# Differential attention prompt heads: a bank each for two small score blocks, the next block's maximum ahead of the mixture, and two buffers for a head's result

## What is computed

```python
def block(args):
    q_blk, i = args
    qpos = i * Q_BLOCK + jnp.arange(Q_BLOCK)
    s = jnp.einsum('bqhcd,bkhcd->bhcqk', q_blk, k, preferred_element_type=jnp.float32) * scale
    w = diff_weights(s, kpos[None, :] <= qpos[:, None], lam_full)      # softmax(s0) - lam * softmax(s1)
    return jnp.einsum('bhqk,bkhe->bqhe', w.astype(v.dtype), v)
...
o = rms_norm(o, subln_g) * (1.0 - lam_init)
return (o.reshape(B, T, ATTN_DIM) * jax.nn.silu(z)) @ w_out
```

## Time and profile before

| | |
|---|---|
| median of 3 runs | 2562.84 us (2559.9 to 2563.27) |
| the profiled execution | 2562.2 us, span 2560.4 us |
| heads 0 to 7 of the prompt | 2008.7 to 2265.7 us of the span |
| projection with the other 56 pages | 2265.7 to 2484.4 us |
| tail (rest of the projection, decode output) | 2484.4 to 2560.4 us |

### The profile page before, as it was taken

The page is one execution under the profiler, slowest core; times in us unless marked ns, Lnnn a source line. Parts: engine busy times, 40 slices in busy tenths (PEclk is TensorE's granted clock), DMA queues, the critical chain, the costliest instruction groups (busy, mean ns, idle before and its releaser), DMA issues.

```text
span 2560.4 us, 51030 instructions
## 1 busy us (share of the span) xinstructions
PE 2472.4 (97%) x20963; PEld 2164.5 (85%) x20963; DVE 1513.4 (59%) x1663; ACT 1016.2 (40%) x1832; POOL 347.5 (14%) x137
## 2 busy tenths in 40 slices
PE   8999999999999999999999999999999987789999
PEld 7999999999999999899999999998999532345565
DVE  4665675665664334455789878877667565643211
ACT  4111211111121223777655467776555334331111
POOL 4323332323321111000000000000000022120000
PEclk9999999999999999999999999999999988889999
DMA  5323323323323332234477787877888999989996
GB/s 155 83 82 97 84 82 91 90 82 87 93 82 87 106 118 91 94 108 159 141 257 271 259 280 245 287 269 265 286 299 295 354 366 388 372 305 376 380 343 221
DMA packets 376326, 520.52 MB, mean 203 GB/s; under 512 B 16553, under 2 KB 311858, under 8 KB 357682
## 3 DMA queue, kind: packets, MB, share of 16 engines
q1 hardware_dynamic: 314434, 461.55, 52.5%
q10 hardware_dynamic: 61600, 56.45, 6.5%
q0 software_dynamic: 128, 0.26, 0.0%
HBM read 483.46 MB, written 34.75 MB: 202 GB/s over the span
## 4 chain that ended last, share of the span: by engine, by line
PE 83%; DVE 5%; ACT 5%; DMA 4%; issue 2%; ACTq 1%; SPq 1%; POOL 0%; DVEq 0%; POOLq 0%
PE psum L112 25%; PE psum L1292 16%; PE psum L120 12%; PE psum L1300 8%; PE psum L1888 7%; PE psum L1343 4%; PE psum L1962 4%; ACT w_raw L1057 1%; DVE h_keys_turned L1235 1%; DMA w_raw<-in_w_in_b_dram 1%; PE psum L1941 1%; PE psum L1308 1%; PE psum L1923 1%; DMA w_raw<-in_w_kv_dram 1%; DVE prompt_probs L1779 1%
## 5 line engine op out<-in xcount | busy, mean ns | idle before, releaser
L1292 PE MATMUL psum<-x_hi,w_hi 128*128 128x272 f32 x2048 | 433.6, 293 | 0.0
L112 PE MATMUL psum<-x_hi,w_hi 128*128 128x272 f32 x2048 | 427.4, 289 | 2.2 <-DVEq L446 2.2
L112 PE MATMUL psum<-x_lo,w_hi 128*128 128x272 f32 x2048 | 426.5, 290 | 0.0
L1292 PE MATMUL psum<-x_lo,w_hi 128*128 128x272 f32 x2048 | 425.3, 289 | 0.0
L1292 PEld LDWEIGHTS psum<-x_hi,w_hi 128*128 128x128 f32 x2048 | 321.4, 189 | 16.6 <-issue 16.5
L112 PEld LDWEIGHTS psum<-x_hi,w_hi 128*128 128x128 f32 x2048 | 321.9, 190 | 2.7 <-issue 2.3
L1292 PEld LDWEIGHTS psum<-x_lo,w_hi 128*128 128x128 f32 x2048 | 321.4, 188 | 0.0
L112 PEld LDWEIGHTS psum<-x_lo,w_hi 128*128 128x128 f32 x2048 | 321.2, 189 | 0.0
L1235 DVE STREAM_TRANSPOSE h_keys_turned<-h_ring 128x1024 f32<-128x1024 f32 x256 | 299.9, 1215 | 22.0 <-DMA h_ring<-in_cache_k_dram 11.1
L399 POOL TENSOR_TENSOR w_raw<-w_raw,params 128x2048 f32<-128x2048 f32 x63 | 240.4, 3817 | 508.5 <-DMA w_raw<-in_w_in_a_dram 508.5
L1300 PE MATMUL psum<-x_hi,w_lo 128*128 128x272 f32 x2048 | 285.3, 294 | 0.0
(11 more groups left out here) (214 smaller groups left out, 3010.4 us busy)
## 6 DMA issues: line engine op xcount, KB each, us to landing
h_ring<-in_cache_k_dram SPq DMA_DIRECT2D x256, 512.0 KB, 6.7
ring<-in_cache_v_dram SPq DMA_DIRECT2D x128, 1024.0 KB, 8.1
w_raw<-in_w_in_a_dram SPq DMA_DIRECT2D x64, 1024.0 KB, 6.1
w_raw<-in_w_kv_dram SPq DMA_DIRECT2D x16, 2048.0 KB, 13.4
w_raw<-in_w_in_b_dram SPq DMA_DIRECT2D x15, 2048.0 KB, 10.0
w_raw<-in_w_out_a_dram SPq DMA_DIRECT2D x16, 1024.0 KB, 5.6
wo_raw<-in_w_out_b_dram SPq DMA_DIRECT2D x8, 2048.0 KB, 12.1
ring<-in_w_out_b_dram SPq DMA_DIRECT2D x16, 1024.0 KB, 7.2
```

The costliest lines, as they stand in the source:

```text
L112: pe.matmul(out[:, g, 0:GT], m.WH[s][:, k * P:(k + 1) * P], x[:, k * T + g * GT:k * T + (g + 1) * GT], start=(k == 0 and x is xh), stop=Fa ...
L1292: pe.matmul(psum[n % 2][:, g, 0:GT], m.WH[n % 2][:, k * P:(k + 1) * P], x[:, k * T + g * GT:k * T + (g + 1) * GT], start=(k == 0 and x is ...
```

## The change

Block 2's scores of both maps go side by side into bank 2 and block 3's into bank 3 (`scores_of`), so that blocks 1, 2 and 3 can be scored once block 0's exponentials are done, without waiting for each other; the next head's block 0 now waits for all exponentials of this head. Maxima, sums and inverses get a column pair for each block. Orders within a head are rewritten on all three engines: VectorE takes block `x + 1`'s maximum ahead of block `x`'s mixture; the next head's first scores move from step 7 to step 6 on TensorE; the sum of squares moves from step 1 to step 2; ScalarE's `norm_o` moves from step 1 to step 4 and `split_y` with `load_gate` from step 5 to step 8. `o` gets a second buffer in the space of the projection's first high weights, so `take_o(r)` waits for head `r - 2`; in return `split_hi(0)` and `split_lo(0)` move to step 8 of the last head, and `split_hi(0)` waits for GpSimd's end of head 6. The turned decode output (`turn_rows`, `take_out`) moves by up to three steps where it would meet the squares in their bank.

```diff
-        self.pmx, self.pden, self.pinv = work(2), work(2), work(2)
+        self.pmx, self.pden, self.pinv = ([work(2) for x in range(TT)] for a in range(3))
...
+    LAST_NORM = 2
...
-        def score_bank(x):
-            return (BB, A)[x % 2]
+        def scores_of(x):
+            n = (rows_of(x) + 1) * P
+            if x < 2:
+                return m.PS[:, (BB, A)[x]:(BB, A)[x] + 2, 0:n]
+            return m.PS[:, BB + x - 2, 0:2 * n].rearrange("p (c n) -> p c n", c=2)
...
+        def turned_at(i):
+            v = (i + 1) * NPG + 1
+            while any(squares_at(r) <= v <= squares_at(r) + (LAST_NORM if r < H - 1 else 0) for r in range(H)):
+                v += 1
+            return v
...
             def split_hi(n):
...
+                    if n == 0:
+                        act.wait_ge(yl_ready, H - 1)
...
             def head_step(r, j):                       # ScalarE
-                if j == 0 and r:
-                    load_inner(r + 1)
-                    square_o(r - 1)
-                if j == 0 and r == H - 1:
-                    split_hi(0)
+                if j == 0:
+                    if r:
+                        load_inner(r + 1)
+                        square_o(r - 1)
+                    prompt_exps(r, 1)
                 if j == 1:
                     prompt_weights(r, 0)
+                    prompt_exps(r, 2)
+                if j == 4:
+                    prompt_weights(r, 1)
+                    prompt_exps(r, 3)
                     if r:
                         norm_o(r - 1)
-                if j == 2:
-                    prompt_exps(r, 1)
-                if j in (4, 6):
-                    prompt_weights(r, j // 2 - 1)
-                    prompt_exps(r, j // 2)
-                if j == 5 and r:
-                    split_y(r - 1)
+                if j == 5:
+                    prompt_weights(r, 2)
                 if j == 7:
                     prompt_weights(r, 3)
-                if j == 8 and r + 1 < H:
-                    prompt_exps(r + 1, 0)
+                if j == 8:
+                    if r + 1 < H:
+                        prompt_exps(r + 1, 0)
+                    if r:
+                        split_y(r - 1)
+                    if r == H - 1:
+                        split_hi(0)
...
             def take_o(r):
                 dve.wait_ge(o_done, r + 1)
-                after(dve, yl_ready, r)
+                after(dve, yl_ready, r - 1)
...
             def head_step(r, j):                       # VectorE
                 if j == 0:
-                    prompt_mix(r, 0)
                     if r:
                         take_o(r - 1)
-                if j == 1 and r == H - 1:
-                    split_lo(0)
-                if j in (2, 4, 6):
-                    prompt_max(r, j // 2)
-                if j in (3, 5, 7):
-                    prompt_mix(r, j // 2)
-                if j == 8 and r + 1 < H:
+                    prompt_max(r, 1)
+                if j == 1:
+                    prompt_max(r, 2)
+                if j == 2:
+                    prompt_mix(r, 1)
+                if j == 3:
+                    prompt_max(r, 3)
+                if j in (4, 5):
+                    prompt_mix(r, j - 2)
+                if j == 6 and r + 1 < H:
                     prompt_max(r + 1, 0)
+                if j == 8:
+                    if r + 1 < H:
+                        prompt_mix(r + 1, 0)
+                    else:
+                        split_lo(0)
...
             def prompt_scores(r, x):
                 if x == 0:
                     pe.wait_ge(inner_in[r % 2], 48 * (r // 2 + 1))
-                    after(pe, prompt_exp, r * (2 * TT) - 2)
+                    after(pe, prompt_exp, r * (2 * TT))
...
                 else:
-                    pe.wait_ge(prompt_exp, r * (2 * TT) + 2 * (x - 1))
+                    pe.wait_ge(prompt_exp, r * (2 * TT) + 2)
...
             def head_step(r, j):                       # TensorE
+                if j == 0:
+                    prompt_scores(r, 1)
                 if j == 1:
-                    if r:
-                        prompt_turn(r, 0)
-                    prompt_scores(r, 1)
-                    if r:
-                        prompt_squares(r - 1)
-                if j == 2 and r == 0:
                     prompt_turn(r, 0)
-                if j in (3, 5):
-                    prompt_scores(r, (j + 1) // 2)
-                if j in (4, 6):
-                    prompt_turn(r, j // 2 - 1)
+                    prompt_scores(r, 2)
+                if j == 2 and r:
+                    prompt_squares(r - 1)
+                if j == 3:
+                    prompt_scores(r, 3)
+                if j == 4:
+                    prompt_turn(r, 1)
+                if j == 5:
+                    prompt_turn(r, 2)
+                if j == 6 and r + 1 < H:
+                    prompt_scores(r + 1, 0)
                 if j == 7:
                     prompt_turn(r, 3)
-                    if r + 1 < H:
-                        prompt_scores(r + 1, 0)
                 if j == 8:
                     prompt_out(r)
```

More of the change, by code:

```diff
@@ L1429, in attend_and_project @@
         yh, yl = sb("ay_hi", [P, KT * SEQ], F32R), sb("ay_lo", [P, KT * SEQ], F32R)
-        with nc.sbuf_tensor("wo_hi_first", [P, D], F32):
+        with nc.sbuf_tensor("o_early", [P, D], F32) as o_even:
             with nc.sbuf_tensor("norm_early", [P, D], F32) as early:
@@ L1433, in attend_and_project @@
         wh = [sb(f"wo_hi{s}", [P, D], F32R) for s in range(2)]
-        o = sb("prompt_o", [P, 1024])[:, :]
+        o_odd = sb("prompt_o", [P, 1024])
         with nc.sbuf_tensor("heads", [P, 7 * 1024], F32) as heads:
@@ L1447, in attend_and_project @@
         pwt = sb("prompt_weights", [P, 2048])[:, :]
+        o = [(o_even[:, 0:1024], o_odd[:, :])[r % 2] for r in range(H)]
         ro = [early[:, 1024:1536]] * (H - 1) + [pwt[:, 1536:2048]]
@@ L1503, in place, with squares_at @@
             return None, None, n, v - STARTS[n]
+        def squares_at(r):
+            return FIRST + 1 if r == H - 1 else (r + 1) * HP + 2
+        def turned_at(i):
[3 more added lines that the diff above has]
+            return v
         @block.sync
@@ L1638, in square_o @@
                 act.wait_ge(o_taken, r + 1)
-                act.activation(osq[r], o, ACT.Square).then_inc(osq_ready, 1)
+                act.activation(osq[r], o[r], ACT.Square).then_inc(osq_ready, 1)
             def norm_o(r):
@@ L1775, in prompt_mix @@
                 dve.wait_ge(prompt_exp, r * (2 * TT) + (2 * x + 2))
-                prompt.link(dve.reciprocal(pinv, pden))
-                prompt.link(dve.tensor_scalar(w[:, SEQ:SEQ + n], w[:, SEQ:SEQ + n], pinv[:, 1:2], m.NLAM[:, 0:1],
+                prompt.link(dve.reciprocal(pinv[x], pden[x]))
+                prompt.link(dve.tensor_scalar(w[:, SEQ:SEQ + n], w[:, SEQ:SEQ + n], pinv[x][:, 1:2], m.NLAM[:, 0:1],
                                               ALU.mult, ALU.mult))
-                dve.scalar_tensor_tensor(out=w[:, 0:n], in0=w[:, 0:n], scalar=pinv[:, 0:1], in1=w[:, SEQ:SEQ + n],
+                dve.scalar_tensor_tensor(out=w[:, 0:n], in0=w[:, 0:n], scalar=pinv[x][:, 0:1], in1=w[:, SEQ:SEQ + n],
                                          op0=ALU.mult, op1=ALU.add).then_inc(prompt_w, 1)
@@ L1823, in seq_step @@
             def seq_step(i, p):
-                if p == 2 and i:
+                if i and i * NPG + p == turned_at(i - 1):
                     take_out(i - 1)
@@ L1838, in _ @@
             prompt_max(0, 0)
+            prompt_mix(0, 0)
             for v in range(NV):
@@ L1905, in turn_rows @@
                 after(pe, out_taken, i)
-                after(pe, o_ln, 2 * min((i + 1) * NPG // HP, H) - 1)
+                after(pe, o_ln, 2 * sum(squares_at(r) <= turned_at(i) for r in range(H)) - 1)
                 for t in range(4):
@@ L1920, in prompt_scores @@
                 else:
-                    pe.wait_ge(prompt_exp, r * (2 * TT) + 2 * (x - 1))
+                    pe.wait_ge(prompt_exp, r * (2 * TT) + 2)
                 for c in range(2):
-                    last = pe.matmul(m.PS[:, score_bank(x) + c, 0:(qb + 1) * P], qh[r % 2][:, c * SEQ + qb * P:c * SEQ + (qb + 1) * P],
-                                     kh[r % 2][:, c * SEQ:c * SEQ + (qb + 1) * P], start=True, stop=True)
+                    last = pe.matmul(scores_of(x)[:, c, :], qh[r % 2][:, c * SEQ + qb * P:c * SEQ + (qb + 1) * P],
+                                     kh[r % 2][:, c * SEQ:c * SEQ + (qb + 1) * P], start=True, stop=True, skip_group_check=True)
                 last.then_inc(prompt_scored, 1)
@@ L1947, in prompt_squares @@
                 pe.wait_ge(osq_ready, r + 1)
-                after(pe, out_taken, ((r + 1) * HP - 1) // NPG)
+                after(pe, out_taken, sum(turned_at(i) < squares_at(r) for i in range(NSEQ)))
                 for e in range(2):
@@ L2004, in seq_step @@
             def seq_step(i, p):
```

(2 more changed lines are left out.)

21 lines of the change are left out of this document (10 added, 11 removed).

## The result

The changed kernel takes 2577.54 us in the median of 11 runs (2567.42 to 2586.89), against 2564.8 us (2557.73 to 2567.88) for the kernel before on the same chip: ratio 1.0051, 95% interval 1.0032 to 1.0069. It is slower by 0.5%, some 13 us. Forecast were 2548 us and a range that ended at 2562. The third rival, starvation, had the sign, with +8 us where some 13 were measured. The profiled execution is the slowest of the runs, 2586.89 us with a span of 2584.3, so its own differences to before are larger than those of the medians; what follows is read for where and why, and the sizes are taken from the timed runs.

The account below looks back on a forecast made before the run. The prediction took a latency chain through three engines to bound the heads, with DMA traffic right below it. Gains of 6.4 (heads 1 to 6), 3 (head 0) and 4.7 us (hand-over) took 2562.2 to 2548 us; range 2536 to 2562.

Parts of the forecast that it names:

- The third rival, starvation: Heads 1 to 6: pages crowd out gate and head data in the other queue; +8 us, 2570 us, chance 0.13.
- The chain bounds the kernel before: Heads before the change: a latency chain through three engines sets the time, 32.2 us a head.
- The chain alone would run at 24.5 us a head: Heads in the new order: without the DMA bound, about 24.5 us a head instead of 32.2.
- At least 176.1 us of DMA in heads 1 to 6: Heads 1 to 6: 74.48 MB at 423 GB/s take 176.1 us, so at most 17.3 us can go.
- TensorE will stand 5 to 9 us for the head's data in heads 1 to 5: Before the next head's first scores: values land after they are needed, so TensorE idles 5 to 9 us each time.
- 1.8 us of idle DMA a head: Heads 1 to 6: a third of the possible 5.5 us idle, giving 186.9 us, a gain of 6.4 us.
- The traffic, named as a sign at near 400 GB/s: Heads 1 to 6 after the change: DMA traffic was to show near 400 GB/s.
- Head 0 gains 3: Head 0: no finished head to carry, its order improves alike; gain 3 us (0 to 4).
- the first rival: Heads and hand-over: the chain gain comes through whole with no DMA idle; -27 us, 2535 us, chance 0.16.
- Head 7 and the hand-over gain 4.7: Last head to first projection matmul: the shorter chain counts, part lost to the weight split; gain 4.7 us.
- Projection and tail unchanged: Projection and tail: TensorE is full, its work is the same and DMA has room; no change.
- The range: Whole kernel: 2536 us (nearly the whole gain) to 2562 us (idle DMA of 3.9 us a head).

Follow-up runs that it names:

- e8: Kernel before, with only a quarter of each of 72 pages loaded and used four times: 2560.71 us, ratio 0.9987.
- e7: Changed kernel, with only a quarter of each of 72 pages loaded and used four times: 2547.5 us, ratio 0.9940.
- e5: Changed kernel, with queries, keys and values of heads 2 to 7 loaded in SyncE's page queue: 2554.69 us, ratio 0.9967.
- e12: Changed kernel, with head data in the page queue, `norm_o` at step 5 and `take_o(7)` before `split_lo(0)`: 2549.41 us, ratio 0.9952.
- e9: Changed kernel, with `take_o(7)` in front of `split_lo(0)` on VectorE: 2574.49 us, ratio 1.0047.
- e2: Changed kernel, with the next head's first scores and their maximum back at step 7: 2568.56 us, ratio 1.0028.
- e3: Changed kernel, with the gate's load issued behind the next head's queries, keys and values: 2576.5 us, ratio 1.0057.
- e10: Changed kernel, with `norm_o` behind weights 2 at step 5 instead of in front at step 4: 2579.14 us, ratio 1.0064.
- e1: Changed kernel, with values counted by their own semaphore, so first scores wait for queries and keys alone: 2559.06 us, ratio 0.9987.

## Why the prediction was wrong, point by point

*The chain bounds the kernel before.* Right: with light pages it stays where it was (e8), and the mixture of 384 columns fell from 2.335 us on average to 0.619. It did not stand behind GpSimd in every head, though: in head 0, which has no finished head to carry, it took 0.62 us before too, and 2.58 in the other seven.

*The chain alone would run at 24.5 us a head.* Too short by 5: e7 shows 29.3. This is a second error, and it made the first one dear. The plan had the chain 4.8 us a head below the DMA floor of 29.3, so a stall would have been half hidden; in truth the chain is as long as that floor, and the table above shows the long stalls added in full. Some heads do run at 23 to 25. In others `take_o` waits behind the decode softmax, and GpSimd's subtraction meets VectorE at step 8. The schedule had put the decode work down as 2 us of TensorE time and not as work in front of `take_o`.

*At least 176.1 us of DMA in heads 1 to 6.* Nothing went below it with all pages: 179.9 us in e5, at 414 GB/s, and 180.0 in e12. That it alone bounds these heads isn't shown, because with light pages the chain takes 175.5 us, nearly the same. The heads of e5 are within 0.9 us of those of e7 one by one, save 2.6 us in head 6. So single heads can run at 25 us with full pages, which the prediction thought forbidden; only their mean can't.

*TensorE will stand 5 to 9 us for the head's data in heads 1 to 5.* The place was right. The size was wrong in its pattern: in the profile 1.75 to 12.43 us in four heads and none in the others. Which heads stall differs from one execution to the next (2, 4 and 6 in e9's profile), but with this order and ScalarE's queue as it was head 6 is always among them: it takes 38 to 43 us in the profiles of the changed kernel, e2, e3, e9 and e10. The 11 runs spread over 19 us, where 6 of e5 spread over 4. That one stall brings on the next, by a ring that is refilled beside the head's data, fits this but isn't shown by itself.

*1.8 us of idle DMA a head.* This is the step that failed. The prediction had both ends, 0 and 5.5 us, and took a third, on the ground that one queue's pause is the other's gain. Total traffic did not protect it: heads 1 to 6 of the profile moved some 75 MB, in 214.4 us instead of 176, which is 6 us a head. The profile of e9 has the same order in these heads and lies near the changed kernel's median, and there they take 209.6 us: 5.6 us a head, the upper end and not a third of it. The length of one such pause was foreseen well, 6.5 us measured against 5.5; what was missed is how often and how fully it comes, and that the chain has no room for it. The traffic, named as a sign at near 400 GB/s, came to 352. The small-packet queue got 0.72 MB against 3.50 with equal packets. Here the rule of the Trainium skill that was cited (DMA: Bandwidth & Descriptors, Queues, rings and completion order) held and should have had the larger weight. The section states the round by packets; that small packets then get few bytes follows from it and is what these counts show. The trace had a warning that was read as a mere bound, the 22.9 us of the earlier trace rows. e1, e5 and e7 take the wait, the second queue or the traffic away in turn, and each takes the loss away.

*Head 0 gains 3.* 0.6 us in the profile. From its first scores to its value product the kernels with the new order take 24.1 to 24.4 us (22.1 in e2), those with the old order 23.8 to 25.2, so there is no gain that stands out. Nor was the term well made: the floor of 27.2 us given for this head allows 3.05 at most, so a gain of 3 took nearly all of it, and the first rival's 26.5 us lies below it.

*Head 7 and the hand-over gain 4.7.* Before 33.35 + 1.36, after 28.75 + 5.58: 0.4 us. In e5 and e7, which have the same order there, the two together take 35.9 and 36.0 us, 1.2 more than before. Head 7 ran 3.7 us longer than laid out, and the hand-over took all the rest; the order at its end (`split_hi(0)`, `split_lo(0)`, `take_o(7)`) was as predicted.

*Projection and tail unchanged.* The stretches of 218.70 and 218.75 us don't begin and end at the same work. From the first projection matmul to the start of the last page's use it is 217.5 us after and 217.0 before, so this part was right. From there to the end of the span it is 79.0 us against 76.4. The four profiles with the old order have 75.6 to 76.4 there, the ten with the new order 75.7 to 80.9. On the chain that ended last a transfer of ScalarE's queue takes 6.25 us in the changed kernel and 6.72 in e5, where it took 5.21, and the 36 projection matmuls behind it 9.78 and 10.11 us instead of 8.20. The prediction put this at nothing; what makes the transfer longer stays open.

*The range.* By the prediction's own terms its end, 2562 us, stands for 4.1 us of idle DMA a head, not 3.9: 7.5 us more in heads 1 to 6 beside the gains of 3 and 4.7.

What stays open: how much the gate in front of the data costs by itself (e3 moved the wait), whether `norm_o` and `take_o(7)` bring anything in e12, and the transfer in the tail.

## What to carry to other kernels

Before a consumer is moved forward, look at when its data land, lay its chain out with everything that stands in front of it on each engine, and count bytes for each queue, not in total. A transfer of small packets beside a stream of large ones in another queue gets a fraction of the traffic as long as the stream has work, and a stall of the consumer gives the stream more work, not less. Putting the urgent load into the stream's own queue, in its place, cost nothing here and turned a loss of 0.5% into a gain of 0.3%. One semaphore for three transfers, of which the first matmul needs two, cost some 16 us here.

## What the runs showed of the hardware that was not expected

In stretches where both had work, two DMA queues were served packet by packet so exactly that their counts agree within 4% (406 to 397 before, 477 to 495 after), at 7.3 KB a packet in one and 1.1 to 1.5 KB in the other. With pages and head data in line in one queue, and only the gates and decode scores beside it, the engines held 414 GB/s over 180 us. And a tiny VectorE operation (L865, 128x32) beside a GpSimd subtraction of 2.35 us took 1.98 us in e7 instead of 0.24 and ended with it. In the changed kernel one took 1.74, and a mixture of 512 columns that started 0.03 us after a subtraction of 2.35 took 2.87 instead of 0.75. In these three cases VectorE lost what was left of GpSimd's operation, whatever the size of its own.
